# Mixture-of-experts encoder: 512 of the 2048 columns of the expert sum move from TensorE to VectorE

## The reference

```python
def peer_ffn(h, w_q, sub_keys, u, v):
    ...
    q = (x @ w_q).reshape(t, PEER_HEADS, 2, PEER_D_HALF)
    scores = jnp.einsum('thcd,cnd->thcn', q, sub_keys).astype(jnp.float32)
    top_s, top_i = lax.top_k(scores, PEER_TOPK)
    ...                       # 16 of 256 candidates per head: idx, gate g
    def one_block(args):
        x_blk, i_blk, g_blk = args
        u_sel = u[i_blk]
        a = jax.nn.gelu(jnp.einsum('tkd,td->tk', u_sel, x_blk), approximate=False) * g_blk
        return jnp.einsum('tk,tkd->td', a, v[i_blk])
```

## Time and profile before

| | |
|---|---|
| median of 3 runs | 3809.72 us (3805.19 to 3812.08) |
| span of the profiled execution | 3811.5 us |
| TensorE busy in it | 3089.0 us, 81% |
| VectorE busy | 1726.9 us, 45% |
| GpSimd busy | 1697.6 us, 45% |
| ScalarE busy | 1009.5 us, 26% |
| feed-forward part of layer 0, of layer 1 | from about 466 to 1839 us, from about 2456 us to the end |

### The profile page before, as it was taken

One profiled execution on the slowest core, in us unless ns is written; L12 is line 12 of the kernel. 1 busy time (PEld: TensorE's weight loads), 2 busy tenths in 40 slices (PEclk: granted clock), 3 DMA queues, 4 the chain that ended last, 5 costly groups with the idle time before them and its releaser, 6 DMA issues.

```text
span 3811.5 us, 33124 instructions
## 1 busy us (share of the span) xinstructions
PE 3089.0 (81%) x9272; PEld 1715.4 (45%) x9272; DVE 1726.9 (45%) x3093; ACT 1009.5 (26%) x2401; POOL 1697.6 (45%) x1145
## 2 busy tenths in 40 slices
PE   7888788888867777777699998788888877777777
PEld 6445644444423322222577876644444433222232
DVE  3333255555545555555311121255555555555554
ACT  3334322222212222221144443222222222222221
POOL 4003455444434444444177665455444444444443
PEclk8877999999988999999699998899999999999999
DMA  4113599999999999999178683599999999999998
GB/s 156 58 58 118 173 417 416 417 417 417 407 415 390 405 413 410 410 411 414 48 170 163 158 147 122 199 417 416 417 417 417 408 387 411 409 411 408 411 406 367
DMA packets 253041, 1242.05 MB, mean 326 GB/s; under 512 B 25888, under 2 KB 63264, under 8 KB 120864
## 3 DMA queue, kind: packets, MB, share of 16 engines
q0 software_dynamic: 147456, 1073.81, 68.3%
q1 hardware_dynamic: 105504, 167.23, 15.9%
HBM read 1238.85 MB, written 2.10 MB: 326 GB/s over the span
## 4 chain that ended last, share of the span: by engine, by line
PE 29%; DMA 28%; issue 23%; DVE 9%; POOL 9%; ACT 2%; SPq 0%; POOLq 0%; DVEq 0%; ACTq 0%
DMA room<-in_peer_u_dram,index 26%; PE psum L906 18%; POOL w_low L545 6%; PE psum L840 3%; POOL room L566 2%; PE psum L628 2%; PE psum L629 2%; PE psum L630 2%; DVE room L1671 2%; DMA room<-in_peer_v_dram,index 1%; ACT diag L1236 1%; POOL room L561 1%; DVE work L1646 1%; DVE work L1650 1%; DVE key_f L1652 1%
## 5 line engine op out<-in xcount | busy, mean ns | idle before, releaser
L906 PE MATMUL psum<-room,diag 128*128 128x512 f32 x4096 | 1939.4, 623 | 593.5 <-ACT diag L1236 584.2
L1671 DVE CUSTOM_DVE_ANT_0 room<-room,normed 128x2048 f32<-128x2048 f32 x512 | 1186.0, 2325 | 1195.0 <-DMA room<-in_peer_u_dram,index 1194.0
L906 PEld LDWEIGHTS psum<-room,diag 128*128 128x128 f32 x4096 | 789.5, 199 | 1667.5 <-issue 947.5
L566 POOL DMA_INDIRECT room<-in_peer_v_dram,index x512 | 571.2, 1116 | 1111.3 <-PE psum L906 560.9
L561 POOL DMA_INDIRECT room<-in_peer_u_dram,index x512 | 643.4, 1257 | 420.0 <-DVE dots L1671 191.2
L545 POOL TENSOR_TENSOR w_low<-wbuf,w_high 128x2048 fp32r<-128x2048 f32 (+1 forms) x108 | 480.8, 4462 | 556.5 <-ACT w_high L982 556.4
L1227 ACT ACTIVATE acts<-dots 128x1 f32<-128x1 f32 x512 | 103.8, 203 | 1903.2 <-DVE dots L1671 1903.2
L982 ACT ACTIVATE w_high<-wbuf 128x2048 fp32r<-128x2048 f32 (+1 forms) x108 | 200.4, 1859 | 279.7 <-DMA wbuf<-in_fox_w_in_dram 142.3
L628 PE MATMUL psum<-w_high,x_high 128*128 128x512 f32 (+1 forms) x608 | 242.5, 399 | 4.3 <-POOL w_low L545 4.3
L629 PE MATMUL psum<-w_low,x_high 128*128 128x512 f32 (+1 forms) x608 | 237.9, 391 | 0.0
L630 PE MATMUL psum<-w_high,other 128*128 128x512 f32 (+1 forms) x608 | 237.9, 391 | 0.0
(11 more groups left out here) (164 smaller groups left out, 1939.6 us busy)
## 6 DMA issues: line engine op xcount, KB each, us to landing
wbuf<-in_fox_w_in_dram SPq DMA_DIRECT2D x64, 1024.0 KB, 7.7
wbuf<-in_peer_w_q_dram SPq DMA_DIRECT2D x64, 512.0 KB, 15.5
wbuf<-in_mla_w_o_dram SPq DMA_DIRECT2D x16, 1024.0 KB, 5.1
wbuf<-in_fox_w_o_dram SPq DMA_DIRECT2D x16, 1024.0 KB, 5.1
wbuf<-in_mla_w_in_dram SPq DMA_DIRECT2D x8, 1024.0 KB, 8.2
wbuf<-in_mla_w_kvb_dram SPq DMA_DIRECT2D x32, 256.0 KB, 3.3
room<-in_peer_u_dram,index POOLq DMA_INDIRECT x512, 15.4
room<-in_peer_v_dram,index POOLq DMA_INDIRECT x512, 14.3
```

The costliest lines, as they stand in the source:

```text
L566: pool.indirect_dma_start(v_ring[:, r, :], None, peer_v.rearrange("l n d -> (l n) d"), bass.IndirectOffsetOnAxis(index[:, p, s:s + 1], 0)) ...
L906: mm = pe.matmul(psum[:, 4 * b + q, :], diag[:, r, :], v_ring[:, r, q * TILE:(q + 1) * TILE], start=False, stop=False, skip_group_check=True)
L1671: V.tensor_tensor_reduce(u_ring[:, r, :], u_ring[:, r, :], normed[:, b, :], 1.0, 0.0, ALU.mult, ALU.add, dots[:, r:r + 1]).then_inc(dot_do ...
```

## The change

The constant `PE_COLS` is 1536. TensorE makes three matmuls for a slot in place of four, over columns 0 to 1535, and `mm_done` counts after the third. A new VectorE instruction `axpy` (a scalar_tensor_tensor of 128 x 512) multiplies columns 1536 to 2047 of the v rows by the weight in `acts[:, 1, r]` and adds them to the same columns of `resid`. It runs one slot late: the order on VectorE is dot(s), axpy(s-1), dot(s+1), axpy(s), and so on; at `choose` it is dot(10), axpy(9), choose, dot(11), axpy(10). The v gather of slot s+4 waits for `axpy_done` of slot s too, and ScalarE's gelu of slot s+4 as well. The final addition and the zeroing take three banks in place of four.

```diff
@@ -63,6 +63,7 @@
 CHOOSE_AT = 11
 COPY_Q_AT = 4
 CHOOSE_STEPS = 24
+PE_COLS = 3 * TILE
 
 
 class Events:
@@ -298,6 +299,7 @@
         u_full = [sem(f"u_full{r}") for r in range(RING)]
         v_full = [sem(f"v_full{r}") for r in range(RING)]
         dot_done, diag_ready, mm_done = sem("dot_done"), sem("diag_ready"), sem("mm_done")
+        axpy_done = sem("axpy_done")
         peer_added = sem("peer_added")
         stored = sem("stored")
 
@@ -562,6 +564,7 @@
                                             bass.IndirectOffsetOnAxis(index[:, p, s:s + 1], 0)).then_inc(u_full[r], 16)
 
                     pool.wait_ge(mm_done, slot + 1)
+                    pool.wait_ge(axpy_done, slot + 1)
                     pool.sem_inc(held["pool"], 1)
                     pool.indirect_dma_start(v_ring[:, r, :], None, peer_v.rearrange("l n d -> (l n) d"),
                                             bass.IndirectOffsetOnAxis(index[:, p, s:s + 1], 0)).then_inc(v_full[r], 16)
@@ -902,7 +905,7 @@
                             pe.wait_ge(diag_ready, slot + 1 + RING)
                             pe.wait_ge(v_full[r], 16 * (number * (SLOTS // RING) + s // RING + 1))
 
-                            for q in range(4):
+                            for q in range(PE_COLS // TILE):
                                 mm = pe.matmul(psum[:, 4 * b + q, :], diag[:, r, :],
                                                v_ring[:, r, q * TILE:(q + 1) * TILE],
                                                start=False, stop=False, skip_group_check=True)
@@ -1224,6 +1227,8 @@
                         r = s % RING
                         slot = number * SLOTS + s
                         act.wait_ge(dot_done, slot + 1 + RING)
+
+                        act.wait_ge(axpy_done, slot + 1)
                         chain.step(nc.scalar.activation(acts[:, 0, r:r + 1], dots[:, r:r + 1], ACT.Gelu))
                         chain.settle()
                         if s == 0:
@@ -1332,6 +1337,7 @@
                 dve.sem_inc(held["dve"], 1)
 
             dve.sem_inc(dot_done, RING)
+            dve.sem_inc(axpy_done, RING)
             dve.sem_inc(pick_used, 1)
 
             def angles():
@@ -1661,18 +1667,34 @@
                 chain.settle()
                 V.tensor_scalar(gates[:, p, :], soft_e[:, :], soft[:, 2:3], None, ALU.mult).then_inc(gate_ready, 1)
 
+            def dot(number, b, s):
+                r = s % RING
+                slot = number * SLOTS + s
+                dve.wait_ge(u_full[r], 16 * (number * (SLOTS // RING) + s // RING + 1))
+
+                dve.wait_ge(diag_ready, slot + 1)
+                V.tensor_tensor_reduce(u_ring[:, r, :], u_ring[:, r, :], normed[:, b, :], 1.0, 0.0,
+                                       ALU.mult, ALU.add, dots[:, r:r + 1]).then_inc(dot_done, 1)
+
+            def axpy(number, b, s):
+
+
+                r = s % RING
+                slot = number * SLOTS + s
+                dve.wait_ge(v_full[r], 16 * (number * (SLOTS // RING) + s // RING + 1))
+                dve.wait_ge(diag_ready, slot + 1 + RING)
+                dve.wait_ge(axpy_done, slot + RING)
+                V.scalar_tensor_tensor(out=resid[:, b, PE_COLS:D], in0=v_ring[:, r, PE_COLS:D],
+                                       scalar=acts[:, 1, r:r + 1], in1=resid[:, b, PE_COLS:D],
+                                       op0=ALU.mult, op1=ALU.add).then_inc(axpy_done, 1)
+
             def slots(number, b, which):
                 for s in which:
-                    r = s % RING
-                    slot = number * SLOTS + s
-                    dve.wait_ge(u_full[r], 16 * (number * (SLOTS // RING) + s // RING + 1))
-
-                    dve.wait_ge(diag_ready, slot + 1)
-                    V.tensor_tensor_reduce(u_ring[:, r, :], u_ring[:, r, :], normed[:, b, :], 1.0, 0.0,
-                                           ALU.mult, ALU.add, dots[:, r:r + 1]).then_inc(dot_done, 1)
+                    dot(number, b, s)
+                    axpy(number, b, s - 1)
 
             def zero_accumulators(b):
-                V.memset(psum[:, 4 * b:4 * b + 4, :], 0.0).then_inc(acc_zero, 1)
+                V.memset(psum[:, 4 * b:4 * b + PE_COLS // TILE, :], 0.0).then_inc(acc_zero, 1)
 
             def peer(layer):
                 first = NB * PHEADS * layer
@@ -1685,7 +1707,7 @@
                 def pair_of_units(i, b, last):
                     for p in range(2):
                         number = first + b * PHEADS + 2 * i + p
-                        slots(number, b, range(CHOOSE_AT))
+                        slots(number, b, range(1, CHOOSE_AT))
                         if not (last and p and b == NB - 1):
                             choose(layer, number + 1, 1 - p)
                         if last and p and b == 0:
@@ -1693,17 +1715,24 @@
                             dve.wait_ge(match_done, PHEADS * (layer + 1) + 1)
                             zero_accumulators(1)
                         slots(number, b, range(CHOOSE_AT, SLOTS))
+                        if not (last and p):
+                            dot(number + 1, b, 0)
+                        axpy(number, b, SLOTS - 1)
 
                 for b in range(NB):
+                    dot(first + b * PHEADS, b, 0)
                     with dve.Fori(0, looped) as i:
                         chain.enter(i, 2 * CHOOSE_STEPS)
                         pair_of_units(i, b, False)
                     chain.leave(looped)
                     pair_of_units(looped, b, True)
 
-                    dve.wait_ge(mm_done, (first + (b + 1) * PHEADS) * SLOTS + RING)
-                    V.tensor_tensor(resid[:, b, :], psum[:, 4 * b:4 * b + 4, :].rearrange("p q n -> p (q n)"),
-                                    resid[:, b, :], ALU.add).then_inc(peer_added, 1)
+                    units = first + (b + 1) * PHEADS
+                    dve.wait_ge(mm_done, units * SLOTS + RING)
+                    dve.wait_ge(axpy_done, units * SLOTS + RING)
+                    V.tensor_tensor(resid[:, b, 0:PE_COLS],
+                                    psum[:, 4 * b:4 * b + PE_COLS // TILE, :].rearrange("p q n -> p (q n)"),
+                                    resid[:, b, 0:PE_COLS], ALU.add).then_inc(peer_added, 1)
 
             norm(0)
             angles()
```

## The result

The changed kernel takes **3826.13 us** (median of 4 runs, 3825.68 to 3830.48) against 3809.89 (3805.19 to 3812.08) before: a ratio of 1.0047, 95% interval 1.0033 to 1.0061. It is slower by 16 us; the forecast was 3815.0, slower by 5. The profiled execution has a span of 3823.9, 12.4 us above.

The account below looks back on a forecast made before the run. The DMA stream bounds steady slots at 4.97 us; choose +13.6, between the blocks -5.0, ends -3.0 and -0.3 sum to +5.3 on a median of 3809.7, giving 3815.0 us. Its own range is 3805 to 3825, with rivals 3793 to 3842.

Parts of the forecast that it names:

- What bounds the kernel: Steady slots: the DMA stream sets 4.97 us a slot and covers TensorE, so TensorE's saving is worth nothing there.
- the reserve of the ring: Steady slots: later u gathers still land in time, price 0; the rival that it fails: 3839 us, chance 0.18.
- Around choose: Behind choose: later axpys delay the gathers v(14), u(15) and v(15), lengthening the hole; +13.6 us over 17 units.
- The price of 0.8 us a unit: Hole behind choose: 3.1 us against 2.3 before, so +0.8 us in each of 17 units.
- one mean hole of 2.3 us: Behind choose in the kernel before: units take 81.8 us against 79.5 for 16 slots, so 2.3 us is a hole.
- the landing of the rows behind v(14): Behind choose: v(14), ready at 16.0 us after dot(10), lands 6.1 later at 22.1, due at 20.0: hole 2.1.
- Between the blocks: Unit 7: fewer matmuls left to work off and shorter addition and zeroing, 2.5 us less per block change, -5.0 in all.
- The ends: Layer ends: fewer last matmuls and a shorter addition, -3.0 us in layer 0 and -0.3 at the very end.
- The clock: TensorE: lower mean clock, below 0.9 in block 1, returning to full clock under full load, at nearly no price.
- In units 0 to 4 ... so 0: Units 0 to 4 of both layers: weight loads share the DMA engines, gathers land later than the hole, cost 0.
- the first: Behind choose: gathers slip through between dot and axpy, -0.4 us a unit, -15 us, 3795; chance 0.22.
- TensorE's clock came back: Steady slots: the rival that TensorE stays at half clock, 5.1 against 4.97 us a slot, 3840 or more; chance 0.10.

Follow-up runs that it names:

- run 4: The changed kernel measured once more, unaltered: 3827.17 us, ratio 1.0046 to the kernel before.
- Run 6: Changed kernel with three matmuls a slot but no axpy and no wait on it (columns 1536 to 2047 left out): 3785.44 us, ratio 0.9938 to the kernel before.
- run 7: Changed kernel with its axpys and their waits, but four matmuls a slot on TensorE as before: 3835.98 us, ratio 1.0075 to the kernel before.
- Run 5: Changed kernel with the axpy of slot 10 moved ahead of choose: 3838.6 us, ratio 1.0075 to the kernel before.
- run 1: Changed kernel with VectorE's loops over pairs of units written out as straight code: 3818.17 us, ratio 1.0030 to the kernel before.
- run 2: The kernel before with VectorE's loops over pairs of units written out as straight code: 3814.82 us, ratio 1.0015 to the unedited kernel before.
- run 3: Changed kernel with 64 semaphore instructions added at the start of VectorE's program: 3832.14 us, ratio 1.0052 to the kernel before.

## Why the prediction was right, and where it was not

**The number: 11 us low, and 1 us above the range that the forecast gave itself (3805 to 3825).** It is not the loads alone. Without the four units the profile would be 1.6 us shorter than before, where the forecast has 5.3 longer: what choose costs was nearly right, and the gains between the blocks and at the very end were put too low. These misses and the loads partly cancel, and that the sum came as near as it did is luck.

**What bounds the kernel: right.** Steady slots stayed at 4.97 us and the DMA row at 9. That TensorE's saving is worth nothing in a steady slot held, and so did the reserve of the ring: a u gather that ends 3 us later costs nothing there.

**Around choose: right in the order of events, a little off in price.** In unit 8 of layer 0 the forecast's times for dots and gathers came out within 0.3 us. The next unit begins at T0+29.6 to 30.8 in the units 8 to 14, and not always at T0+30 or later. The price of 0.8 us a unit measured +0.9 on average over the units 5, 6 and 8 to 14 of both layers without the units 10 and 12 of layer 1, and the same in run 4; but that mean is carried by the units 5 and 6 (+0.8 to +1.5) and unit 8 of both layers (+1.8 and +5.3). In layer 0 the units 9 to 14 have +0.5 on average, between -1.4 and +1.9; in layer 1 the units 9, 11, 13 and 14 have 0 on average. What the working mis-sized is the hole itself: it set one mean hole of 2.3 us against a longer one. There are two holes before, and the change lengthens the first (in unit 10 of layer 0 the dot(0) of the next unit comes 32.1 us after dot(10), 30.7 before; in unit 11 32.1 and 31.2) and closes the second (runs 6 and 7). Run 5 showed besides that the landing of the rows behind v(14) does not set it, as the working had it; what fits is the release of v(15) and of those behind it. Why unit 8 of layer 1 has a slot of 7.7 us right after the blocks change is open; runs 1 and 6 have it too (7.6).

**Between the blocks: right in sign, too small.** -7.4 and -4.3 against -2.5 each; the additions' wait for TensorE fell from 35.3 us in all four to 9.5:

```profile
L1733 DVE TENSOR_TENSOR resid<-psum,resid 128x1536 f32<-128x1536 f32 x4 | 7.0, 1758 | 9.5 <-PE psum L909 9.5
```

Part of it is given back in the unit behind (+1.8, +5.3): -4.6 for both pairs of units 7 and 8, where the forecast has -3.4.

**The ends: right in layer 0, missed in layer 1.** The end of layer 0 was forecast at -3.0 and measured -2.9. The forecast's 10.1 us for eighteen records are 9.68 here:

```profile
1834.96 9.68 PE L909 MATMUL psum<-room,diag 128*128 128x512 f32 x18 [19.68 <-ACT diag L1241]
```

At the end of layer 1 the last six records ran at the full clock in 2.84 us, and unit 15 had no long slot, where the kernel before has 6.19 us behind its dot(0) and 5.47 at the last: -2.9 against -0.3.

**The clock: right in a steady slot.** Its mean fell to 0.82 in block 1. Of 82 bursts of six records between 1140 and 1800 us, 51 took 2.84 us and 31 took 4.1 to 4.5, so TensorE came back to the full clock after one slow slot, and the slots stayed at 4.97 us. Run 6, fast at 0.863, and run 7, slow at 0.921, show that the clock does not make the loss; what it costs where TensorE catches up behind choose was not measured by itself. In the time line the bursts are longer than the idle time in front of them (2.84 against 0.93, 4.54 against 2.19 us), mostly every second or third is slow, and in these 660 us no two slow ones follow each other. That TensorE starts at half clock behind choose held: in the kernel before, both feed-forward parts have 35 idle times of over 5 us on TensorE, and the granted share in the first us behind them is 0.50 in all 35.

**The missed step: "In units 0 to 4 ... so 0", and a sum in which no term stands for the code.** I costed 512 axpys by their time on VectorE, and by whom they hold up, and not by the room of their instructions. The loop body of VectorE grew from 225 to 322 records, and in two of four loops instruction blocks then came again in every turn. The first unit of such a turn was 2.7 to 5.0 us longer: 14 us, more than the whole difference from the forecast (11). Runs 1 to 4 show it: gone in straight code, moved by code ahead of it, repeated in another run. The blocks come in the first slots of a turn and again later in it (3 and 2 of the five in layer 0, 2 and 3 in layer 1), and the time is not lost in a stop of VectorE: in the slot shown in run 3 the rows of u, asked for 13.7 us before the load, land about 1 us late, and the dot starts 0.02 us behind them. I had not asked of the loop whether its code would be loaded again.

Of the rivals, the first came in part, where it changes nothing. In the changed kernel 110 gathers that start within 0.045 us of a dot's start are done in 0.94 us, and it is the dot that takes longer (2.32 to 2.37 us); nearly all of them are u gathers of the steady slots. The 294 that start later in a dot are held until 0.81 us after its end, as forecast. What in a gather is held, a read or the making of its descriptors, no trace shows: they show when its instruction ends, and those words of the forecast are my reading. TensorE's clock came back (from 1140 to 1800 us no two slow slots in a row), and the ring's reserve held. The range, 3793 to 3842, held the time by its allowance for rivals that did not decide it: the cause that did was in none of them.

## What to carry to other kernels

Count the instructions of a loop body as a resource of the engine that runs it: look at the packets of the instruction queues inside a loop before and after, since 64 against 38 was the only mark of 14 us on the page, and every stalled slot was signed by a DMA of data, which did land late. Where a stream of gathers bounds a kernel, ask which instruction releases the next gather and move long work out of its way: cutting choose in three gave 1.3%, while moving work from TensorE to VectorE, both idle for a part of every steady slot of block 1, lost. And when an edit has two parts, run each alone; here one was a gain of 22 us and the other a loss of 29.

## What the runs showed of the hardware that was not expected

Packets on the queue q14 can come again in the turns of a VectorE loop, and slots with such a packet are longer more often than slots without. In the changed kernel q14 has 64 packets of 8 KB (0.52 MB; 38 and 0.31 MB before), five of them in each of the second and third turns of two of the four loops. The first unit of such a turn takes 89.3 and 90.6 us in layer 0 (+3.5 and +5.0 on the kernel before) and 84.7 and 84.2 in layer 1 (+2.7 and +2.9). With 64 instructions ahead at the start of VectorE's program (run 3) the window from 640 to 740 us has no packet on q14 where the changed kernel has four, the window from 1330 to 1490 has five where it has none, and the units 2 and 4 of layer 0 take 85.6 and 85.7 us, the units 10 and 12 84.1 and 84.0 (81.6 and 82.5 in the changed kernel).

In the slots 2 to 9 of the units 9 to 15 of all thirteen traces, 31 of 68 slots with a packet on q14 and 28 of 43 with one on q8 alone were longer than 5.12 us, and 2 of 1345 without. With q14, 24 of the 31 were 0.9 to 1.0 us over 4.97; with q8 the 28 were 0.2 to 1.5 over it. In the slot shown in run 3 the rows that came late had been asked for 13.7 us before the packet.

A granted clock that changes from slot to slot leaves the slots of the DMA stream at 4.97 us: in the changed kernel six records take 2.84 us in 51 bursts and 4.1 to 4.5 in 31 (granted share 0.82 on average from 1140 to 1800 us).

Which comes first decides between a gather's instruction and a dot product of 2048 columns. Of the gathers of the changed kernel that start inside a dot, the 294 that start 0.045 us or more behind the dot's start end 0.81 us after its end (they take 1.57 to 3.06 us in place of 0.94), and the 110 that start closer are done in 0.94, while the dot takes 2.32 to 2.37 us in place of 2.29.
